# Sixteen gate products moved from VectorE to GpSimd in the closing stages of a hybrid backbone step

## The reference, cut to what matters

```python
hs = modulate(rmsnorm(xs, norm_mix_pre[layer]), mod_s[0], mod_s[1])
...
xs = xs + mod_s[2] * rmsnorm(ys, norm_mix_post[layer])
hs = modulate(rmsnorm(xs, norm_ffn_pre[layer]), mod_s[3], mod_s[4])
xs = xs + mod_s[5] * rmsnorm(sq_relu_mlp(hs, w_ffn_in[layer], w_ffn_out[layer]), norm_ffn_post[layer])
```

## Time and profile before

| | |
|---|---|
| time, median of 3 runs | 1505.16 us (1502.3, 1505.16, 1505.34) |
| span of the profiled execution, first to last instruction | 1499.1 us |
| median above that span | 6.1 us |
| busy, TensorE / VectorE / ScalarE / GpSimd | 95% / 48% / 36% / 37% |
| mean granted clock of TensorE | 0.990 |

### The profile page before, as it was taken

How to read it: one execution, slowest core, us unless ns; L and a number is a source line. 1 busy time by engine, 2 the same in 40 slices (tenths; PEclk the granted TensorE clock), 3 DMA queues, 4 the chain that set the end, 5 groups by cost and what they waited for, 6 DMA issues and landing times.

```text
span 1499.1 us, 19717 instructions
## 1 busy us (share of the span) xinstructions
PE 1422.2 (95%) x7958; PEld 1205.9 (80%) x7958; DVE 717.2 (48%) x1274; ACT 545.7 (36%) x912; POOL 549.4 (37%) x383
## 2 busy tenths in 40 slices
PE   5999999899999999999899889998999999999998
PEld 3876877789889899898667755677989989989986
DVE  5477945532544544545834677617323223222236
ACT  4467706522122122123631466628312212222222
POOL 1431404534244244244334234433624424433430
PEclk8999999999999999999999999999999999999999
DMA  9524253345334234233425000030534213213201
GB/s 353 144 94 143 86 193 104 112 128 112 108 104 141 90 108 141 87 111 119 162 90 170 28 1 1 1 112 29 165 103 127 65 48 113 80 44 103 85 28 71
DMA packets 95026, 153.76 MB, mean 103 GB/s; under 512 B 10764, under 2 KB 49368, under 8 KB 94936
## 3 DMA queue, kind: packets, MB, share of 16 engines
q1 hardware_dynamic: 82432, 145.76, 29.7%
q10 hardware_dynamic: 12504, 6.75, 1.8%
HBM read 149.58 MB, written 2.92 MB: 102 GB/s over the span
## 4 chain that ended last, share of the span: by engine, by line
PE 76%; DVE 8%; ACT 4%; issue 2%; POOL 2%; DMA 2%; DVEq 0%; ACTq 0%
PE PS L1493 23%; PE PS L1495 23%; PE PS L1494 23%; POOL WL L1068 2%; PE PS L1792 1%; PE PS L1784 1%; PE PS L1544 1%; DVE GG L1458 1%; DVE X L1230 1%; PE PS L1642 1%; PE PS L1759 1%; DVE XCB L1226 1%; ACT WH L812 1%; DVE HL L1265 1%; DVE RAW L678 1%
## 5 line engine op out<-in xcount | busy, mean ns | idle before, releaser
L1068 POOL TENSOR_TENSOR WL<-RAW,WH 128x512 fp32r<-128x512 f32 x340 | 468.3, 1413 | 719.3 <-ACT WH L812 701.7
L1493 PE MATMUL PS<-HH,WH 128*128 128x384 f32 (+1 forms) x1152 | 357.9, 311 | 8.4 <-POOL HL L1058 3.6
L1495 PE MATMUL PS<-HH,WL 128*128 128x384 f32 (+1 forms) x1152 | 356.2, 309 | 0.0
L1494 PE MATMUL PS<-HL,WH 128*128 128x384 f32 (+1 forms) x1152 | 356.1, 309 | 0.0
L812 ACT CAST WH<-RAW 128x1024 fp32r<-128x1024 f32 x170 | 169.1, 1047 | 445.3 <-PE PS L1495 331.2
L1493 PE MATMUL PS<-WH,AH 128*128 128x512 f32 x640 | 250.4, 391 | 0.3 <-DVE AL L1282 0.3
L1495 PE MATMUL PS<-WH,AL 128*128 128x512 f32 x640 | 249.5, 390 | 0.0
L1494 PE MATMUL PS<-WL,AH 128*128 128x512 f32 x640 | 249.3, 390 | 0.0
L1493 PEld LDWEIGHTS PS<-HH,WH 128*128 128x128 f32 x1152 | 218.9, 190 | 16.7 <-issue 10.3
L1494 PEld LDWEIGHTS PS<-HL,WH 128*128 128x128 f32 x1152 | 219.1, 190 | 0.6
L1495 PEld LDWEIGHTS PS<-HH,WL 128*128 128x128 f32 x1152 | 218.7, 190 | 0.0
(11 more groups left out here) (210 smaller groups left out, 1624.0 us busy)
## 6 DMA issues: line engine op xcount, KB each, us to landing
RAW<-in_w_mod SPq DMA_DIRECT2D x43, 1024.0 KB, 5.1
RAW<-in_w_ffn_in SPq DMA_DIRECT2D x32, 1024.0 KB, 5.5
RAW<-in_w_ffn_out SPq DMA_DIRECT2D x32, 1024.0 KB, 4.9
RAW<-in_w_in_even SPq DMA_DIRECT2D x7, 1024.0 KB, 5.3
RAW<-in_w_qkv SPq DMA_DIRECT2D x6, 1024.0 KB, 5.2
RAW<-in_w_out_even SPq DMA_DIRECT2D x4, 1024.0 KB, 5.1
GG<-gates ACTq DMA_DIRECT2D x16, 256.0 KB, 3.8
RAW<-in_w_out_odd SPq DMA_DIRECT2D x4, 1024.0 KB, 5.9
```

The lines of the kernel that those rows point to most:

```text
L1068: ins = nc.gpsimd.tensor_tensor(cut(ring_view(WL, ld, j)), cut(w_view(ld, b)), cut(ring_view(WH, ld, j)).bitcast(f32), ALU.subtract)
L1493: MM(out, wh, xh, start=first, stop=False)
L1494: MM(out, wh, xl, start=False, stop=False)
L1495: return MM(out, wl, xh, start=False, stop=last)
```

## The change

In each of the four closing stages GpSimd makes the product of ACC and GG for tiles 0 to 3, and VectorE only that of tile 4. The waits that stood before the product on VectorE go along with it, in the new function `closing_ready`. GpSimd has this work in its list at the step `post`, ahead of the splits of that step and behind those of the steps before. VectorE still waits for `yg_ready` before it adds to X.

```diff
+        def gain_of(ph, t):
+
+            return GG[:, (0 if ph in (1, 3) else 2) + (t > 0), :]
+
+        def closing_ready(eng, s):
+
+            ph, t = s["ph"], s["t"]
+            if ph % 2:
+                upto(eng, b_free, s["yb"])
+                upto(eng, b_free, s["yb"] - TT)
+            else:
+                upto(eng, b_free, s["yb"] - 1)
+                upto(eng, b_free, s["yb"])
+                eng.wait_ge(a_lo, 16 * ph)
+            chains = TT * (ph - 1) + t
+            if chains:
+                eng.wait_ge(x_new, chains)
+            for half in (0, 1):
+                eng.wait_ge(gg_in[half], 32 * ph)
...
+                if k == "post" and s["t"] < TT - 1:
+                    closing_ready(pool, s)
+                    nc.gpsimd.tensor_tensor(YG, ACC[:, s["t"], :], gain_of(s["ph"], s["t"]), ALU.mult).then_inc(yg_ready, 1)
...
-                    y_in_acc(s)
-                    if ph % 2 == 0:
-                        dve.wait_ge(a_lo, 16 * ph)
-                    if nchain > 1:
-                        dve.wait_ge(x_new, nchain - 1)
-                    if t == 0:
-                        for half in (0, 1):
-                            dve.wait_ge(gg_in[half], 32 * ph)
-                    gain = GG[:, (0 if ph in (1, 3) else 2) + (t > 0), :]
-                    V_.tensor_tensor(YG, ACC[:, t, :], gain, ALU.mult).then_inc(yg_ready, 1)
+                    if t == TT - 1:
+                        closing_ready(dve, s)
+                    if t == TT - 1:
+                        V_.tensor_tensor(YG, ACC[:, t, :], gain_of(ph, t), ALU.mult).then_inc(yg_ready, 1)
                     dve.wait_ge(ysum, nchain)
```

More of the change, by code:

```diff
@@ L1135, in vec_rows @@
                     ins.then_inc(vec_read if kt == 3 else vec_step, 1)
[L1137 to L1144, removed]
             nmod = nchain = nkt = nscale = 0
```

## The result

The changed kernel takes 1514.52 us (median of 4 runs, 1512.14 to 1516.79) against 1505.25 of the kernel before (1502.3 to 1507.1). The ratio is 1.0061, with a 95% interval of 1.0042 to 1.0079: 9.2 us slower, 6.3 to 11.9. The forecast was slower, 1516.7 us in a range of 1509.5 to 1519.5. The profiled execution took 1512.14 us and spans 1510.2, 11.1 us more than the span before.

A forecast was written before the change was run, and what follows sets the result against it. The prediction took TensorE, busy 95% of the span, and its waits around the closing stages to bound the kernel. Terms 4.7 + 2.1 + 4.7 + 0 = 11.5 us gave 1516.7 us, range 1509.5 to 1519.5.

The forecast's parts named there:

- The queue: After each mixer, GpSimd's product for tile 0 stands behind four subtractions, so ScalarE's first square of X comes 3.8 us later.
- The price: One 128x1024 product on GpSimd takes 2.35 us, within bounds of 1.89 and 2.53, against 1.22 us on VectorE.
- The lock at tile 1: After each mixer, VectorE's ACC write holds SBUF exclusively and delays GpSimd's product: 4.83 us from copy to square, not 3.65, +1.2.
- Tiles 2 and 3, -0.3 us: After each mixer, these tiles take 4.83 us from copy to square against 4.99 or about that: -0.3 for both together.
- No slack behind the mixer stages: TensorE already waits for the cut of tile 1 after each mixer, so the 4.7 us of delay stay, each time.
- Stage 2, +2.1 us: Closing stage after the first MLP: SBUF waits at tile 2 delay X and the PART copy; 2.1 us reach TensorE.
- The first part: After the first MLP, tile 2: the modulation's small operations wait for GpSimd's product, +2.2 less the 1.2 us VectorE saves.
- The second part: After the first MLP, tile 2: GpSimd's cut of tile 0, at 727.35, holds SBUF and X waits 1.2 us more.
- The third, 0.2 for the rest: The closing stage after the first MLP costs 0.2 us if engines do not wait for each other at SBUF.
- The cover on TensorE: After the first MLP, TensorE waits until 715.29 for the w_mod transfer, hiding tile 0's lateness of about 1.6 us.
- Stage 4, 0: Closing stage after the second MLP: the next first sum ends at 1475.65, TensorE wants its bank by 1476.00; cost 0.
- The base: The 11.5 us were added to the median of 1505.16, leaving its 6.1 us above the span of 1499.1 as is.

## Why the prediction was right, point by point

- **The queue, +3.8 us at tile 0 of stages 1 and 3**: right, 3.74 in the trace, 3.75 and 3.73 with only these two products moved, and gone when the product goes ahead of the splits.
- **The price, 2.35 us**: right, 2.37 to 2.41. The softmax scaling, from which the lower bound of 1.89 was worked out, is cheaper per element. The prediction puts a product of 2.25 us at 0.5 us off the sum; by its own terms it is 0.9, for 0.1 us less counts at each of four tiles in two stages, and once in stage 2.
- **The lock at tile 1, +1.2 us**: right, 1.10. The product ended 3.32 us after the copy's start (253.21 - 249.89; forecast 3.44), 2.24 after the end of VectorE's ACC write and not the full 2.4.
- **Tiles 2 and 3, -0.3 us**: -0.43 in stage 1 (4.41 less 3.74 and 1.10).
- **No slack behind the mixer stages**: right. From the MLP's first matmul of stage 1 to the first sum of stage 2 are 439.96 us before and 439.94 after. From that of stage 3 to the first sum of stage 4 they are 431.88 and 433.40, 1.52 more; 1.42 of it is a lower clock (last section), for which the prediction had no term.
- **Stage 2, +2.1 us**: the size was near (1.8), its parts were not, and that is luck.
  - The first part was right: the small operations wait as forecast, and from the first sum of tile 2 to its X update are 5.44 us instead of 4.50, +0.94 where 2.2 less 1.2 was forecast.
  - The second part, that GpSimd's cut then holds the lock at 727.35 and delays X by a further 1.2 us, is wrong: that cut came late as well, since ScalarE's cast to HH waits for VectorE's half of HF (1.19 us idle before it), and X found the lock free.
  - The third, 0.2 for the rest, was too small: it came to 0.84. Tile 0's product makes the first sum of tile 1 2.04 us late on VectorE (11.74 us after the stage's first sum instead of 9.70). VectorE catches up 1.2 of it, because it no longer waits 1.87 us for the w_mod product behind these sums, and 0.84 are left at the first sum of tile 2 (19.33 instead of 18.49).
  - The cover on TensorE that the prediction counted on held: its matmuls behind the w_mod product start 12.57 us after the first sum instead of 12.72, although they wait 1.06 us for VectorE, since the transfer came earlier (it is issued as the last subtraction ahead of it ends, and that subtraction no longer lost 1 us to VectorE).
  - What was overlooked is the next wait: the prediction names one wait of 0.23 us for VectorE in this stage, but TensorE also waited 0.58 us at 723.49 and 0.69 at 739.99 for the reduction L1201. Where VectorE was already waited for, its 0.84 us went through.
- **Where stage 2's cost goes.** The time of the kernel with stages 2 and 4 only doesn't show it (at most 0.8 us). Behind the stage, the third copy of attention values comes 60.75 us after the first sum in the kernel before, 60.94 in the changed one. But in the kernel before TensorE's clock had fallen there: the stretch has 0.66 of the granted clock. The windows of the kernel before (length, busy time of the five rows, granted clock, DMA share, GB/s):

```profile
757.00:760.00 3.00, 3.00 (x9) 2.45 (x10) 1.38 (x5) 2.27 (x6) 0.70 (x1) 0.66 0.21 79
760.00:765.00 5.00, 5.00 (x30) 3.87 (x30) 1.85 (x5) 0.64 (x2) 1.29 (x1) 0.86 0.00 0
```

  From the cast that ends the stage to that copy are 24.20 to 24.26 us in seven of the nine profiles, whatever was moved. They are 25.80 in the kernel before and 25.52 with stages 1 and 3 only, the two whose clock fell 52 to 58 us after the first sum. The kernel with tile 0 only has the same two waits of TensorE there as the kernel before (1.92 and 0.91 us) and kept its clock; it reaches the copy at 58.99. The four profiles with stage 2 changed as a whole reach it at 60.60 to 61.00, and 60.01 without tile 2's product. So the stage costs 1.6 to 2.0 us at full clock, and executions differ by about as much by where the clock falls. Whether the moved products make a fall at this place rarer is open: of the four profiles with the products of stage 2's tiles 0 to 2 on VectorE two had it, and of the five others none (the kernel with stages 2 and 4 only had one 8 us earlier, and no delay of this copy from it).
- **Stage 4, 0**: +0.35. The term that was mis-sized is the cover: I took the second sum's start as the point at which TensorE wants the bank, and it wants it 0.2 us before, at 1475.80. So the cover was 0.15 on the forecast's own times (1475.80 - 1475.65) and not 0.35, and the sum started 4.53 us after the tile's second sum (1485.85 - 1481.32) instead of the forecast 4.39, with the product at 2.40 and its hand-overs. That used it up.
- **The base.** I put the sum on the median and took the 6.1 us between it and the span as lying around the span. The changed kernel's profiled execution took 1512.14 us at a span of 1510.2: only 1.9 us lie around it. The other 4 us are, by that estimate, how much quicker the profiled execution of before was than the median. The forecast's time doesn't hang on this, since 11.5 was added to a median. It is 2.2 above 1514.52 because 11.5 is 2.2 above the measured 9.3 (9.2 by the ratio, whose interval goes to 11.9).

The sum of the stages in the changed trace is 4.41 + 1.77 + 4.52 + 0.35 = 11.05 us, beside 11.5 forecast. The span grew by 11.1, but that the two agree is in part chance: the changed execution was 0.56 us late before stage 1, gained 2.00 between stages 2 and 3, where the other's clock had fallen, and lost 1.52 behind stage 3, where its own did. The time grew by 9.2 (6.3 to 11.9). What is shown is the mechanism of the mixer stages, which carry the loss (10.4 us alone). Stage 2's part is seen in the traces and not in the time: with stages 2 and 4 only, the stages are 1.8 us longer and the time at most 0.8, and with the product ahead of the splits they are 4.7 us longer and the time 2.6 (0.6 to 4.5). So in each of these two about 2 us of the stages are missing from the time, and their cause is open; where the clock falls is a possible one. That the total came out right may owe something to luck: a term that the prediction lacked (the clock behind a mixer stage, 1.4) and one that the time doesn't show (stage 2, 2.1) go against each other.

## What to carry to other kernels

An engine that is 37% busy is not free at the moment that matters: before moving an operation to it, read what stands ahead of it in that engine's own list at that place, since work that is issued in order is priced by its place in the queue first and by its duration second. Here two thirds of the loss was two products behind four subtractions, and changing their order took most of it away. Where VectorE and GpSimd both work on SBUF, a long instruction on one can lengthen the shortest on the other (0.16 to 2.25 us here), so look for small operations on the critical path beside it. And where an engine is relieved, check that it doesn't simply wait for the result, as VectorE did here for 3.71 us.

## What the runs showed of the hardware that I had not expected

**A lower clock in one of two like stages.** From the MLP's first matmul to the first of its second part (the matmul over 384 columns) are 15.01 us in both mixer stages of the kernel before. In the changed kernel they are 15.01 in stage 1 and 16.43 in stage 3. The windows of the changed kernel there, in the order of those above:

```profile
1036.00:1042.00 6.00, 6.00 (x30) 4.96 (x29) 5.13 (x9) 5.64 (x14) 3.98 (x2) 1.00 0.00 0
1042.00:1045.00 3.00, 1.08 (x9) 0.79 (x7) 2.81 (x2) 2.64 (x7) 1.42 (x2) 1.00 0.00 0
1045.00:1048.00 3.00, 2.80 (x14) 2.80 (x15) 2.96 (x8) 2.94 (x8) 0.00 (x0) 0.61 0.00 0
```

TensorE had stood still for 2.13 us (busy 1.08 of 3 us) and then ran partly at 1.2 GHz instead of 2.4 (granted clock 0.61). All five profiled kernels with the products of tiles 0 to 3 in the mixer stages have 16.41 to 16.45 us in exactly one of the two, stage 1 or 3, and 15.0 in the other; none of the four without them has it in either. So some 1.4 us of the changed kernel's time is likely clock, on top of the waits that the prediction counted; in the two profiles compared here it stands against the kernel before's own fall behind stage 2. The wait of 2.00 us in stage 1 of the same execution did not bring the clock down, nor did one of 2.47 us at the same place in stage 3 of the kernel with tile 0 only. Why one of two like stages and not the other, no run here tells.

**The lock was paid in full, and the relief came off it.** The Trainium skill, "SBUF — State Buffer", section "Who interferes with whom", has the order of issue decide who waits, and says that the wait is for the whole instruction. The 2.25 us of L1223 and the return of this operation to 0.16 once the product was taken away agree with that. Stage 2 paid 0.9 us for this product, which is the 2.1 us of waiting less the 1.22 us that VectorE no longer spent on it: where both stand in one engine's list on the critical path, they are to be subtracted from each other.
